# Turning the input by 32x32 squares on VectorE, in place of 128x128 transposes on TensorE, in a hybrid pool, convolution and attention block

## What is computed

```
h = rms_norm(x, ln_g[l])
proj = jnp.einsum('bsd,de->bse', h, w_in[l])
...
scores = jnp.einsum('bnqkgd,bnskd->bnkgqs', qb, kb).astype(jnp.float32)
...
y_attn = sliding_window_attention(q, k, v, attn_sinks[l])
```

## Time and profile before

| | us |
|---|---|
| three runs | 1439.57, 1440.66, 1440.68 |
| median | 1440.66 |
| the profiled execution's own time | 1439.26 |
| its span in the profile | 1437.5 |
| TensorE busy | 1414.5 |
| VectorE busy | 1145.6 |
| ScalarE busy | 512.6 |
| GpSimd busy | 386.5 |

### The profile page before, as it was taken

One profiled execution on the slowest core, in us unless ns is written; L12 is line 12 of the kernel. 1 busy time (PEld: TensorE's weight loads), 2 busy tenths in 40 slices (PEclk: granted clock), 3 DMA queues, 4 the chain that ended last, 5 costly groups with the idle time before them and its releaser, 6 DMA issues.

```text
span 1437.5 us, 20200 instructions
## 1 busy us (share of the span) xinstructions
PE 1414.5 (98%) x7024; PEld 1160.5 (81%) x7024; DVE 1145.6 (80%) x2313; ACT 512.6 (36%) x1253; POOL 386.5 (27%) x627
## 2 busy tenths in 40 slices
PE   6999999999999999999999999999999999999998
PEld 5878787887878787878888888888888888888886
DVE  5676757575766757577989998989899988988886
ACT  5544444445445444342112121221122243333332
POOL 4414233322324242120011010110100255555552
PEclk9999999999999999999999999999999999999999
DMA  7326070616143240817033032230327666555531
GB/s 252 129 70 253 11 279 10 255 44 232 61 166 126 79 170 10 312 34 229 1 132 122 40 132 74 87 131 15 132 88 283 259 211 199 172 160 164 160 119 73
DMA packets 79102, 196.82 MB, mean 137 GB/s; under 512 B 14400, under 2 KB 41408, under 8 KB 71360
## 3 DMA queue, kind: packets, MB, share of 16 engines
q1 hardware_dynamic: 64480, 181.40, 34.3%
q10 hardware_dynamic: 14560, 14.68, 3.8%
HBM read 114.27 MB, written 81.79 MB: 136 GB/s over the span
## 4 chain that ended last, share of the span: by engine, by line
PE 90%; DVE 7%; ACT 1%; issue 1%; DMA 1%; POOL 0%; SPq 0%; POOLq 0%; DVEq 0%; ACTq 0%
PE wide L252 13%; PE wide L254 13%; PE wide L253 12%; PE pair L252 12%; PE pair L253 12%; PE pair L254 12%; PE pair L966 3%; DVE m_tail L1723 3%; PE wide L996 2%; PE wide L997 2%; PE turn L953 2%; PE turn L254 2%; PE turn L253 2%; PE turn L252 2%; PE turn L230 1%; DVE x_first L1820 1%
## 5 line engine op out<-in xcount | busy, mean ns | idle before, releaser
L1723 DVE SCALAR_TENSOR_TENSOR m_tail<-m_tail,m_taps 128x512 f32<-128x512 f32 x480 | 338.3, 751 | 4.6
L252 PE MATMUL pair<-xT,w_hi 128*128 128x512 f32 x632 | 255.0, 403 | 5.9 <-DVE xT L245 4.2
L253 PE MATMUL pair<-xT,w_lo 128*128 128x512 f32 x632 | 247.4, 391 | 0.0
L254 PE MATMUL pair<-xT,w_hi 128*128 128x512 f32 x632 | 247.1, 391 | 0.0
L107 POOL TENSOR_TENSOR pool_carrier<-pool_carrier 128x1 f32<-128x1 f32 x83 | 25.7, 310 | 613.6 <-DVE m_meanvar L1732 398.3
L1476 POOL TENSOR_TENSOR operand_sums<-m_y 128x512 f32<-128x512 f32 x75 | 102.0, 1360 | 167.8 <-PE wide L254 116.7
L252 PEld LDWEIGHTS pair<-xT,w_hi 128*128 128x128 f32 x632 | 119.2, 189 | 32.3 <-DVE a_q L864 4.8
L254 PEld LDWEIGHTS pair<-xT,w_hi 128*128 128x128 f32 x632 | 118.9, 188 | 25.6
L253 PEld LDWEIGHTS pair<-xT,w_lo 128*128 128x128 f32 x632 | 119.4, 189 | 20.6
L252 PE MATMUL wide<-xT,w_hi 128*128 128x512 f32 x328 | 128.4, 392 | 0.0
L254 PE MATMUL wide<-xT,w_hi 128*128 128x512 f32 x328 | 127.7, 389 | 0.0
(11 more groups left out here) (240 smaller groups left out, 2926.3 us busy)
## 6 DMA issues: line engine op xcount, KB each, us to landing
xT_scratch<-xT SPq DMA_DIRECT2D x16, 2048.0 KB, 15.7
xs<-in_x_dram SPq DMA_DIRECT2D x32, 512.0 KB, 6.4
x_first<-xT_scratch SPq DMA_DIRECT2D x16, 1024.0 KB, 7.6
xT<-xT_scratch SPq DMA_DIRECT2D x16, 1024.0 KB, 9.1
combo_scratch<-stage SPq DMA_DIRECT2D x28, 512.0 KB, 3.2
m_y<-y_scratch ACTq DMA_DIRECT2D x14, 1024.0 KB, 6.6
y_scratch<-y_out SPq DMA_DIRECT2D x8, 1024.0 KB, 5.9
y_scratch<-y_out SPq DMA_DIRECT2D x16, 512.0 KB, 2.9
```

Source lines behind the costliest of these rows:

```text
L252: nc.tensor.matmul(out, w_hi, x_hi, start=first, stop=False)
L253: nc.tensor.matmul(out, w_lo, x_hi, start=False, stop=False)
L254: return nc.tensor.matmul(out, w_hi, x_lo, start=False, stop=last)
L1723: nc.vector.scalar_tensor_tensor(out=conv[:, i, :], in0=h[:, i, j:j + TB], scalar=taps[:, i, j:j + 1], in1=conv[:, i, :], op0=ALU.mult, op ...
```

## The change

Channels are laid on partitions in another order: tile k, partition 32b + r holds channel 256b + 32k + r (before: tile k, partition p holds channel 128k + p). Weights and gain are loaded in the same order, by four DMAs in place of one. For blocks 1 to 7, x is loaded so that partition 32b + s holds, for 16 groups of 32 tokens, the 256 channels of quarter b of token s of each group (four DMAs of 32 partitions). A transpose of each 32x32 square on DVE then gives the layout that the products want.

- **Load:** SP stores the first half of the block's h, then loads the next x behind the last low split (not behind the transposes), waits for it, and stores the second half.
- **Squares:** of 16 groups of 256 values per partition, ACT squares 8 (before q_hi 1) and DVE 8 (tensor_tensor_reduce, after output 3). A row's sum is spread over four partitions, so TensorE adds them with one 128x128 by 128x16 product (fold_sums, in q2 after channel tile 1); DVE adds epsilon (mean), POOL takes the root.
- **Scale:** ACT, 16 instructions of 128x256 in place of POOL's four of 128x1024, in four parts (after q_hi 2, after the combos' splits, after q_hi 3, after the copy of v).
- **Turn:** DVE, four vector.transpose of 128x1024 in place: after combos of q2, after q_lo 3, after the last combos, and in round 0 between the two invert.
- **Splits:** read xs in SBUF directly, in steps of 32 values. ACT makes high parts 0 to 4 of the next block in round 3, once g3 has used the old ones (semaphore spent); DVE makes low parts 0 to 3 in round 3 behind gate_make and ahead of the second invert. The others stand at the start of the next block. Projection k waits for each high and low part.
- **Output 2** of the last round is copied by ACT (start of the next block), no longer by DVE; POOL's gate_output waits for it.
- **turn_v** stands between the two halves of scores(n, 0), no longer in g0.
- **Block 0** keeps its transposes on TensorE. Its scaling writes to another tile in the new channel order; block 1 is scaled on ACT in rounds 0 and 1 and turned on DVE in rounds 1 and 2 of block 0, two parts each. Four more small POOL instructions make the fold matrix. The gain and the sinks share a semaphore, so the first high split waits for both.
- The stage's last block is written out after the loop on TensorE.

```diff
     def load(self, sp, n):
-        need(sp, self.turned, KT * n)
+        if n == 0:
+            for s in range(SUB):
+                sp.dma_start(self.xs[:, s, :], self.x[0, s * P:(s + 1) * P, :]).then_inc(self.loaded[s], 16)
+            return
+        if n == 1:
+            sp.wait_ge(self.turned, KT)
+        else:
+            sp.wait_ge(self.lo_done, KT * n)
+        width = D // SUB
+        for b in range(SUB):
+            sp.dma_start(self.groups[b * self.SQUARE:(b + 1) * self.SQUARE],
+                         self.x[0, n * TB:(n + 1) * TB, b * width:(b + 1) * width].rearrange("(a s) c -> s a c", s=self.SQUARE)
+                         ).then_inc(self.loaded[b], 16)
...
+    def square(self, act, n):
+        width = D // SUB
+        self.wait_loaded(act, n)
+        for i in range(self.HALF):
+            act.wait_ge(self.squared, SUB + self.HALF * (n - 1) + max(i - SUB + 1, 0))
+            self.nc.scalar.activation(self.squares[:, i % SUB * width:(i % SUB + 1) * width], self.groups[:, i, :], ACT.Square,
+                                      accum_out=self.sumsq[:, i:i + 1]).then_inc(self.squared, 1)
...
+            self.nc.vector.tensor_tensor_reduce(out=out, in0=self.groups[:, a, :], in1=self.groups[:, a, :], scale=1.0, scalar=0.0,
+                                                op0=ALU.mult, op1=ALU.add,
+                                                accum_out=self.sumsq[:, a:a + 1]).then_inc(self.squared_more, 1)
...
+    def fold_sums(self, pe, n):
+
+        pe.wait_ge(self.ident_ready, 8)
+        pe.wait_ge(self.squared, SUB + self.HALF * n)
+        pe.wait_ge(self.squared_more, self.HALF * n)
+        self.nc.tensor.matmul(self.turn[0][:, 0:self.GROUPS], self.fold[:], self.sumsq[:], start=True,
+                              stop=True).then_inc(self.rstd_steps, 1)
...
+    def scale(self, act, n, part):
+
+        act.wait_ge(self.rstd_steps, self.chain(n, 3))
+        for a in range(part * SUB, (part + 1) * SUB):
+            last = self.nc.scalar.activation(self.groups[:, a, :], self.groups[:, a, :], ACT.Copy, scale=self.rstd[:, a:a + 1])
+        last.then_inc(self.rstd_steps, 1)
+
+    def turn_squares(self, dve, n, part):
+
+        dve.wait_ge(self.rstd_steps, self.chain(n, 4 + part))
+        tokens = self.xs[:, part]
+        self.nc.vector.transpose(tokens, tokens).then_inc(self.turned, 1)
...
     def load(self, sp, c):
         matrix, first, _ = self.plan[c]
-        sp.dma_start(self.landing[c], matrix[0, :, first:first + CHUNK].rearrange("(k p) c -> p k c", p=P)).then_inc(self.loaded[c], 16)
+        rows, width = P // SUB, D // SUB
+        for b in range(SUB):
+            sp.dma_start(self.landing[c][b * rows:(b + 1) * rows],
+                         matrix[0, b * width:(b + 1) * width, first:first + CHUNK].rearrange("(k r) c -> r k c", k=KT)
+                         ).then_inc(self.loaded[c], 16)
...
         def body(n):
+            store_xT(n, 0)
             st.load(sp, n + 1)
...
-            store_xT(n)
+            st.wait_loaded(sp, n + 1)
+            store_xT(n, 1)
...
+                if name == "k":
+                    pe.wait_ge(st.hi_done, KT * n + kk + 1)
+                nc.tensor.matmul(out, w_hi, st.hi[:, kk, :], start=(kk == 0), stop=False)
+                nc.tensor.matmul(out, w_lo, st.hi[:, kk, :], start=False, stop=False)
                 if name == "k":
                     pe.wait_ge(st.lo_done, KT * n + kk + 1)
-                last = split3(nc, bank_of(n, p), w.hi(c)[:, kk, cols], w.lo(c)[:, kk, cols], st.hi[:, kk, :],
-                              st.lo[:, kk, :], kk == 0, kk == KT - 1)
+                last = nc.tensor.matmul(out, w_hi, st.lo[:, kk, :], start=False, stop=(kk == KT - 1))
+                if name == "g3" and kk < st.AHEAD:
+                    last.then_inc(st.spent, 1)
...
             if first:
                 st.first_transposes(pe)
-            else:
-                for kk in range(TURNS):
-                    if kk == 2:
-                        need(pe, score_taken, 8 * n)
-                    st.transpose(pe, n, kk)
...
             for j in range(SUB):
-                scores(n, j)
+                scores(n, j, turn_v if j == 0 else None)
```

More of the change, by code:

```diff
@@ L173, in square, with use @@
[L173 to L178, removed]
+        self.spent = sem("xT_spent")
+    def use(self, turn, squares, more_squares, ident, ident_ready, first_rows):
+        self.turn, self.squares, self.more_squares = turn, squares, more_squares
+        self.ident, self.ident_ready, self.first_rows = ident, ident_ready, first_rows
@@ new lines, in wait_loaded, with load_gain @@
+    def wait_loaded(self, engine, n):
+        for b in range(SUB):
+            engine.wait_ge(self.loaded[b], 16 * n + 16)
+    def load_gain(self, sp):
+        width = D // SUB
+        with self.nc.allow_non_contiguous_dma(reason="1024 values, once"):
+            for b in range(SUB):
+                sp.dma_start(self.gain[b * self.SQUARE:(b + 1) * self.SQUARE],
+                             self.ln_g[0, b * width:(b + 1) * width].rearrange("(k r) -> r k", k=KT)).then_inc(self.vectors_loaded, 16)
@@ L196, in first_scale @@
             dve.wait_ge(self.rstd_steps, 2 * s + 2)
[L197 to L211, removed]
+            out = self.first_rows[:, s].rearrange("p k (b r) -> p k b r", b=SUB)
@@ L610, in sync @@
         load_xT(sp, x_first, x_first_loaded, xT_scratch, 0, (3,))
-        store_xT(NB - 1)
+        for piece in range(PIECES):
+            store_xT(NB - 1, piece)
         store(NB - 2)
@@ L696, in scalar @@
     def scalar(act):
-        st.square(act, 0)
+        st.first_square(act)
         w.split_hi(act, CHUNK_K, 0)
@@ L730, in body @@
             first, final = isinstance(n, int) and n == 0, isinstance(n, int) and n == NB - 1
-            for kk in range(KT):
+            for kk in range(0 if first else st.AHEAD, KT):
                 st.split_hi(act, n, kk)
@@ L753, in body @@
                 w.split_hi(act, CHUNK_Q + 1)
+            elif not final:
+                st.square(act, n + 1)
             q_hi(n, 1)
@@ L758, in body @@
                 w.split_hi(act, CHUNK_G)
-            if not final:
-                st.square(act, n + 1)
             q_hi(n, 2)
+            if not first and not final:
+                st.scale(act, n + 1, 0)
             for s in combos.of_block(n, (2,)):
@@ L764, in body @@
             if first:
+                st.square(act, 1)
                 w.split_hi(act, CHUNK_G + 1)
-            if final:
+            elif final:
                 w.split_hi(act, CHUNK_CB)
+            else:
+                st.scale(act, n + 1, 1)
             q_hi(n, 3)
+            if not first and not final:
+                st.scale(act, n + 1, 2)
             for s in combos.of_block(n, (3, 4)):
@@ L781, in body @@
                 exps(n, j, 0)
+                if j == SUB - 1 and not final:
+                    for kk in range(st.AHEAD):
+                        st.split_hi(act, n + 1, kk)
                 if j:
@@ L786, in body @@
                     gate_tanh(n, j)
+                if first and j < 2:
+                    st.scale(act, 1, 2 * j)
+                    st.scale(act, 1, 2 * j + 1)
                 if final and j == 2:
@@ L891, in body @@
             first, final = isinstance(n, int) and n == 0, isinstance(n, int) and n == NB - 1
-            for kk in range(KT):
+            for kk in range(0 if first else PIECE, KT):
                 st.split_lo(dve, n, kk)
-                if not first and kk == 1:
-                    output(n - 1, 2, (n - 1, slot("o2")))
             if first:
@@ L998, in scores, with folding, once @@
                 last.then_inc(score_full, 1)
+                if between and kv == 0:
+                    between()
+        def folding(n):
+            def once(kk):
+                if kk == 1:
+                    st.fold_sums(pe, n + 1)
+            return once
         def turning(m, j):
```

191 lines of the change are left out of this document (131 added, 60 removed).

## The result

Time after: 1470.35 us, the median of 4 runs (1468.64 to 1471.76), against 1440.19 before. The ratio is 1.0209, with a 95% interval from 1.0191 to 1.0227. The change makes the kernel slower by 30 us, where the prediction had 1429.0 and a range up to 1438.5. The profiled execution took 1470.4 with a span of 1468.7.

The account below looks back on a forecast made before the run. PE was taken as the bound, busy 1414.5 of 1437.5 us. Per block 4.0 - 0.2 - 1.3 - 0.4 - 0.1 = 2.0; seven make 14, less 2.5 once is 11.5, so 1440.66 falls to 1429.2 us, range 1416.5 to 1438.5.

Parts of the forecast that it names:

- New wait 2, the fold: At the fold in q2, PE waits for squares of the next x: 0 to 1.0 us a block, taken as 0.4.
- The second term of the same step: DVE's eight squares before the fold, slowed beside POOL's gate_output: 6.6 us against some 5.8 available, 0.8 late.
- What leaves PE: Transposes at block start (2.2 us) and in projection k (1.8) go: 4.0 us saved in each of blocks 1 to 7.
- The fold's product: One added 16-column product on PE per block, between 0.1 and 0.5 us, taken as 0.2.
- New wait 1: In projection k, PE waits for DVE's low splits, slowed beside POOL's scaling: 0.45 to 2.1 us a block, taken as 1.3.
- New wait 3, v: turn_v's earlier transposes make PE wait for the copy of v: 0 to 0.7 us a block, taken as 0.1.
- Turns in block 0: Two turns a round before the second invert in rounds 1 and 2 delay probabilities: 1.5 us once (0 to 3).
- rival C: Slower: DVE's turn takes about 1.95 us or more, delaying probabilities; at half rate, 2.2 us, total 1447.7; chance 0.08.
- The start: First high split waits for the sinks' DMA, with six more DMAs ahead of it: 1.0 us once (0 to 3).
- The second stage: Begins when the first stage ends; taken as unchanged in length and only earlier.
- Rival B: Gain given back: all waits at their upper ends, -0.1 us a block, about 1443, or 1440 with half; chance 0.12.
- rival A: Other engines keep up: wait only 0.45 in projection k, none at fold and v; 3.35 a block, 1418.7; chance 0.24.

Follow-up runs that it names:

- twoq: Changed kernel with quarters 0 and 1 of x loaded on SP's queue, 2 and 3 on ACT's; 1464.66 us, ratio 1.018.
- x128: Changed kernel with each of the four loads of x filling all 128 partitions, same bytes in other places; 1451.79 us (one run).
- fill: Changed kernel with 14 products of 128x512, results unused, on TensorE ahead of each fold; 1458.34 us, ratio 1.0134.
- nogate: twoq with gate_output's multiplications on POOL left out but for one element; 1432.98 us (one run).
- foldv: Changed kernel with squares, scaling and turns later and the fold moved from q2 into v; 1440.91 us, ratio 1.0012.
- both: Changed kernel with the edits of twoq and foldv together; 1435.01 us, ratio 0.9964.
- gateonly: Changed kernel, x on one queue, with gate_output's multiplications on POOL left out but for one element; 1458.0 us (one run).
- best: The kernel of both, with half of the first weights also on ACT's queue; 1434.57 us, ratio 0.9959.

## Why the prediction was wrong

**The step that failed is "New wait 2, the fold".** It said that x "lands about 15 after the start", from SP's issue some 6.5 after projection k's start and a landing of 8 to 9. The issue came a little sooner (269.26 to 274.58, 5.3), and output 3 was right: it begins at 16.5 and ends at 17.2, where I had its end at 16 to 17. But the load took 15.9, so x lands 21.2 after the start. I had the rate from the earlier trace rows, whose DMAs fill 128 partitions in pieces of 4 KB, and took it over for DMAs that fill 32 in pieces of 1 KB. The diff says both. The upper end of the term, 1.0, left no room for a late landing, and the measured wait is 3.7.

**The second term of the same step was undersized too.** The squares beside gate_output were put at 6.6, and they take 6.7 in twoq (283.90 to 290.62) and 7.2 in x128; alone they step by 0.35, 2.8 for eight. What was wrong is the time that they have. I gave them 5.8, from output 3's place before the change. But output 3 is set by DVE's own list and stayed 16.5 behind projection k's start, while PE, freed of four groups of transposes, came to the fold 1.8 sooner: in twoq output 3 ends at 283.2 and PE stands at the fold from 287.5, 4.3 later. So even with x in time the fold waits about 3, not 0.4 (2.9 in x128, where x is in time; in twoq it is still 0.7 late for DVE). The term gave PE its gain and forgot to take it from the slack.

**What no step had: the clock.** A wait was priced at its own length. In the kernel after, stretches of 3.4 to 13.7 us at 0.50 begin in or just behind all the fold's waits but the 2.9 of block 2, and those for y_out and m_sums. In each, about half of the time that PE works is lost. fill, where one such stretch is left, puts this at 12 us. In round terms the span's 31.2 is: saving -27.7 (7 x 3.95); the fold's waits 26.8; y_out's 5.6; half clock 15 (half of the 30 us that PE works at 0.50 in the first stage); start 3.3; second stage 4.5; fold products 1.4. That sums to 29, and 2 are left unexplained.

**y_out in block 1** was not foreseen either. SP queues the raw rows of w_out for the combos behind x there, and DVE waited 8.51 for them:

```profile
125.08 0.69 DVE L477 TENSOR_TENSOR stage_sum<-raw 128x512 f32<-128x512 f32 x1 [8.51 <-DMA raw<-in_w_out_dram]
```

I had written that SP's wait for x holds "the combo stores by some 6 us, off the path", and had not looked at what else x itself is ahead of on the queue. With x in sooner the wait for y_out is 1.3 (x128) and 2.5 (twoq).

The other steps, one by one:

- **What leaves PE, 4.0 a block:** right, 3.95 in the last step.
- **The fold's product, 0.2:** right in size. It steps 0.2 (279.36 to 279.55 in nogate), with the next product 0.1 longer.
- **New wait 1, 1.3 a block:** 0. DVE's splits beside POOL's scaling took 2.88 and 2.74 for four, the 0.70 of before. It is POOL that waited: its four, 1.41 before, take 2.36 and 2.92, as DVE's and then POOL's timelines show. The collision was there, and I had put its price on the wrong engine. Here the nearest row, 1.49 beside GpSimd's scaling, did not carry over. The 0.45 of PE's own lateness did not show either.

```profile
268.73 2.88 DVE L328 SCALAR_TENSOR_TENSOR xT<-xs,a_gain,xT 128x512 fp32r<-128x512 f32 x4
...
271.81 2.74 DVE L328 SCALAR_TENSOR_TENSOR xT<-xs,a_gain,xT 128x512 fp32r<-128x512 f32 x4
```

```profile
268.05 2.36 POOL L759 TENSOR_SCALAR a_rows<-a_rows,a_inv 128x128 f32<-128x128 f32 x4
...
272.56 2.92 POOL L759 TENSOR_SCALAR a_rows<-a_rows,a_inv 128x128 f32<-128x128 f32 x4
```

- **New wait 3, v, 0.1:** 0 in the kernel after. **Turns in block 0, 1.5:** 0.
- **The turn, 1.15 to 1.2, and rival C (1.95 or more):** DVE's groups have it at 1.23, so C falls.

```profile
L290 DVE STREAM_TRANSPOSE xs<-xs 128x1024 f32<-128x1024 f32 x28 | 34.4, 1232 | 0.2
```

- **The start, 1.0:** 3.3, because of the weights, not of the sinks (for them ACT waited 0.43).
- **The second stage, "unchanged":** 4.5 longer, from the weights' loads again: 2.6 of wait for m_sums, and 3.4 us at half clock behind it.
- **Rival B's sum:** -0.1 for each of seven blocks and -2.5 make 1443.9, not "about 1443".

My test for being wrong in the main was met by the second stage, off by over 2 us. Its other half, an unnamed wait over 1 us a block, was not: y_out's 5.6 in block 1 is 0.8 a block over seven, and the fold's wait was named, but put at 0.4. No rival ended near 1470: the only slow one hung on the turn. The mechanism of rival A did come, in foldv and both (75.9 a step, for the 75.6 I gave it), once the fold stood where its squares were ready. Their times, 1440.9 and 1435.0, are far from its 1418.7, because the start, blocks 0 and 1 and the second stage kept their losses.

## What to carry to other kernels

When a diff changes which partitions a DMA fills and how long its pieces are, price the load anew: a row with the same bytes is not the same load. Put a tiny product that gathers other engines' results as late in TensorE's program as its consumer allows, since here a wait of 3 to 4 us cost up to 2.9 more in clock (6.8 at half clock, 1.1 to 1.3 of it under the wait). And when an experiment removes a cause and the wait stays, look for a second one of the same size behind it before giving the theory up.

## What the runs showed of the hardware

- 1 KB packets take 46 ns (median) when a DMA fills 128 partitions and 91 when it fills 32, at 292 and 195 GB/s with the engines full both times (x128, after). Two queues, each filling another 32, brought x's packets to 53 ns and its load from 15.9 to 12.5 us (twoq).
- When a DVE instruction with two SBUF inputs meets POOL, either can be the one held up. The squares went from 0.41 to 1.50 beside multiplications of 128x512; the low splits kept 0.70 beside scalings of 128x128, and those went from 1.41 to 2.92 for four.
- TensorE's granted clock fell to 0.50 in or behind most waits of 1.8 to 6.1 us once the kernel was under way, and the stretches lasted 3.4 or 6.8 us (13.7 where two waits stood close together). It did not fall behind one wait of 2.9 in the kernel after and two each in x128 and gateonly, nor behind some of 1.5 to 2.0 (foldv, x128, twoq, gateonly, nogate, best). Where products of no use filled the wait for the fold, it stayed at 1.00 (fill).
